# Two blocks with their layers written out, part of layer 2's modulation moved into layer 1, and the second block's first weights loaded inside the first block

## The reference

```
mod = silu(c) @ w_mod[l] + b_mod[l]          # 6 vectors of 1024: shifts, scales, gates
h = rms_norm(x) * (1 + sc_m) + sh_m
x = x + g_m * mixer(h)                       # projections w_in, three branches, w_out
u = rms_norm(x) * (1 + sc_f) + sh_f
x = x + g_f * (routed experts(u) + shared expert(u))   # 64 experts, top 8 of 4 groups
```

## Time and profile before

| | |
|---|---|
| median of the runs | 2278.68 us (2278.5 to 2287.8) |
| the profiled execution's own time | 2280.89 us |
| its span | 2279.2 us, 1.7 us less |
| PE busy | 2142.2 us (94%) |
| mean granted TensorE clock | 0.978 |
| DVE, ACT, POOL busy | 976.2, 512.4, 59.3 us |
| moved by DMA | 599.17 MB, mean 263 GB/s |

### The profile page before, as it was taken

One profiled execution on the slowest core, in us unless ns is written; L12 is line 12 of the kernel. 1 busy time (PEld: TensorE's weight loads), 2 busy tenths in 40 slices (PEclk: granted clock), 3 DMA queues, 4 the chain that ended last, 5 costly groups with the idle time before them and its releaser, 6 DMA issues. The chain is left out here.

```text
span 2279.2 us, 35703 instructions
## 1 busy us (share of the span) xinstructions
PE 2142.2 (94%) x13338; PEld 1243.4 (55%) x13405; DVE 976.2 (43%) x2063; ACT 512.4 (22%) x1080; POOL 59.3 (3%) x143
## 2 busy tenths in 40 slices
PE   4999998899999999979999988999999998799998
PEld 2844444556565655547454445565565654366475
DVE  2574323444444444337634144444444444152153
ACT  2133111122222222223232111222222222113122
POOL 1000002000000000000000030000000000110000
PEclk8999999999999999989999999999999999798999
DMA  8652734599999999876536427999999994731621
GB/s 290 207 208 91 295 111 166 213 380 380 388 370 387 379 383 379 323 281 194 194 109 250 178 119 282 382 374 387 377 383 380 382 384 186 244 97 39 221 67 55
DMA packets 165292, 599.17 MB, mean 263 GB/s; under 512 B 13052, under 2 KB 17760, under 8 KB 130656
## 3 DMA queue, kind: packets, MB, share of 16 engines
q1 hardware_dynamic: 163808, 595.10, 68.9%
q0 software_dynamic: 1408, 3.10, 0.6%
HBM read 597.11 MB, written 1.05 MB: 262 GB/s over the span
## 5 line engine op out<-in xcount | busy, mean ns | idle before, releaser
L1103 PE MATMUL banks<-weight_ring,h_t 128*64 128x256 f32 x4224 | 481.8, 381 | 3.3 <-DVE h_t L1836 3.3
L1103 PEld LDWEIGHTS banks<-weight_ring,h_t 128*64 128x64 f32 x4224 | 298.4, 137 | 173.9 <-issue 40.0
L769 PE MATMUL banks<-weight_ring,h_t 128*128 128x512 f32 x768 | 335.8, 593 | 5.3 <-DMA weight_ring<-in_w_in 3.2
L769 PEld LDWEIGHTS banks<-weight_ring,h_t 128*128 128x128 f32 x768 | 145.1, 190 | 188.1 <-issue 182.9
L1862 DVE SCALAR_TENSOR_TENSOR conv_t<-banks,slot_weight,xn 128x512 f32<-128x512 f32 x132 | 99.2, 751 | 293.6 <-ACT xn L1397 293.6
L1091 PEld LDWEIGHTS banks<-z,sp_ 128*128 128x128 bf16 x3168 | 180.5, 99 | 57.2 <-issue 49.2
L1091 PE MATMUL banks<-z,sp_ 128*128 128x128 bf16 x3168 | 202.7, 221 | 6.4 <-DVEq L1826 6.4
L1143 PE MATMUL banks<-xn,conv 128*128 128x512 bf16 x726 | 169.5, 382 | 9.2 <-DVE xn L1867 5.8
L1397 ACT ACTIVATE xn<-banks,slot_weight 128x512 bf16<-128x512 f32 x132 | 90.7, 687 | 342.8 <-PE banks L1130 342.8
L2103 PE MATMUL banks<-weight_ring,h_t 128*128 128x512 f32 (+2 forms) x384 | 136.7, 516 | 11.2 <-DMA weight_ring<-in_w_in 9.6
L1842 DVE TENSOR_TENSOR z<-banks,z 128x128 f32<-128x128 f32 x132 | 38.5, 292 | 229.8 <-ACT z L1382 229.8
(11 more groups left out here) (471 smaller groups left out, 2071.2 us busy)
## 6 DMA issues: line engine op xcount, KB each, us to landing
weight_ring<-in_w SPq DMA_DIRECT2D x264, 1024.0 KB, 10.5
weight_ring<-in_w_in SPq DMA_DIRECT2D x36, 2048.0 KB, 12.9
slots<-in_w SPq DMA_DIRECT2D x68, 1024.0 KB, 8.2
weight_ring<-in_w_mod SPq DMA_DIRECT2D x24, 2048.0 KB, 10.0
qk<-in_w SPq DMA_DIRECT2D x32, 1024.0 KB, 7.0
z<-in_w SPq DMA_DIRECT2D x32, 1024.0 KB, 11.5
weight_ring<-in_w_out SPq DMA_DIRECT2D x8, 2048.0 KB, 7.8
weight_ring<-in_w_in SPq DMA_DIRECT2D x10, 1024.0 KB, 7.8
```

Of the source, the lines that this page charges most:

```text
L769: mm = nc.tensor.matmul(bank[:, 0:cols], stationary[:, k, t * P:(t + 1) * P], w[:, k, 0:cols], start=(k == 0), stop=(k == KT - 1))
L1103: mm = nc.tensor.matmul(h_bank[g * SLOTS:(g + 1) * SLOTS, 0:FF], x_blk[:, j // 2, k, own], w13(j)[:, :, k, g * (FF // 2):(g + 1) * (FF // 2)],
```

## The change

1. All layer loops are written out (`for l in range(DEPTH)`), so that what a wait compares with is a constant. Bank and slot semaphores are shared by both blocks; the 16 increments at the second block's start are gone.
2. Lists are made per layer. `w_mod` chunks 0 to 3 of layer 2 (named 12 to 15) are loaded and used at the end of layer 1: part 12 ahead of `mT`, part 13 behind it, sum 12 and part 14 behind `wo`, sum 13 and part 15 behind the turn, sums 14 and 15 behind `rt`. DVE folds 12 and 13 behind `modulate(1)`, 14 and 15 in the middle of the routing. Layer 2 starts with `ug`.
3. The parameters are in three groups: `load_mod_params` (6 loads) behind `mod` 3, `load_conv_params` (4) behind `ua`, `load_other_params` (10) behind `kc`; layer 2's are issued in layer 1 behind the last `expert2` ahead of the experts' loop. The `vec` turn stands behind `ua`, DVE's `lam` lines behind the stick-breaking part, and the waits are split accordingly.
4. The second block's first four chunks (5 loads, since `n0` has two halves) are issued at the end of the first block's SP program, each when `h_done` says that the last experts have left its slot.
5. The shared expert's first product no longer waits for all four banks; the first layer's `block_count` has three register loads instead of five.

```diff
@@ bank_plan, lists
+MOD_NEXT = {"merged": [("part", 12)], "mT": [("part", 13)], "wo": [("sum", 12), ("part", 14)],
+            "turned": [("sum", 13), ("part", 15)], "rt": [("sum", 14), ("sum", 15)]}
+def chunks_1(layer):
+    first, following = layer == 0, layer + 1 < DEPTH
+    return (
+        mod_chunks(*range(MOD_FIRST if first else 0)) + [(n, (n, 1)) for n in ("ug", "ua", "qc", "kc")]
...
+        + branch_chunks(0) + branch_chunks(1) + mod_chunks(*((12, 13) if following else ()))
+        + [(("wo", h), ("wo", h, 1)) for h in range(2)] + mod_chunks(*((14, 15) if following else ())) + [("shared", None)]
+    )
@@ first_block, SP
-            with sp.Fori(0, DEPTH) as l:
+            for l in range(DEPTH):
                 one = ds(l, 1)
-                pairs_before = [sp.value_load(K.pairs_before[0:1, i, ds(l, 1)], ...
+                if l > 0:
+                    pairs_before = [sp.value_load(K.pairs_before[0:1, i, ds(l, 1)], ...
...
                     if name == ("mod", MOD_FIRST - 1):
-
-                        parameters(one)
+                        load_mod_params(one)
+                    if name == "ua" and l == 0:
+                        load_conv_params(one)
+                    if name == "kc" and l == 0:
+                        load_other_params(one)
...
                 expert2(l, 3, 3)
+                if l + 1 < DEPTH:
+
+                    sp.wait_ge(chosen_ready.sem, chosen_ready.at(l))
+                    sp.sem_inc(wait_carrier, 1)
+                    load_mod_params(ds(l + 1, 1))
+                    load_conv_params(ds(l + 1, 1))
+                    load_other_params(ds(l + 1, 1))
...
+            for s in range(RING):
+
+                sp.wait_ge(h_done, (pairs_before[0] + pairs_before[1]) * 2 + (s % 2 + RING - 1))
+                load_chunk_2(sp, A, K, 0, CHUNKS_2[s][0], s)
@@ first_block, PE
                 mod("start")
 
-                pe.wait_ge(params.sem, params.at(l, params.n))
-                bank = begin("vec", l)
...
                 norm_turn(0, l)
...
+                by_columns("ug")
+                by_columns("ua")
+
+                pe.wait_ge(conv_params.sem, conv_params.at(l, conv_params.n))
+                bank = begin("vec", l)
...
+                mod("merged")
                 pe.wait_ge(merged_ready.sem, merged_ready.at(l))
...
+                mod("mT")
                 pe.wait_ge(mt_ready.sem, mt_ready.at(l))
...
+                mod("wo")
                 norm_turn(1, l)
+                mod("turned")
                 pe.wait_ge(ht_ready[1].sem, ht_ready[1].at(l, 3))
+                pe.wait_ge(other_params.sem, other_params.at(l, other_params.n))
...
+                mod("rt")
@@ first_block, DVE
                 norm_x(0, l)
-                mod(range(MOD_FIRST))
-
-                dve.wait_ge(params.sem, params.at(l, params.n))
+                if l == 0:
+                    mod(range(MOD_FIRST))
+
+                dve.wait_ge(mod_params.sem, mod_params.at(l, mod_params.n))
                 mod_columns(0)
                 modulate(0, l)
...
                 modulate(1, l)
+                if l + 1 < DEPTH:
+                    mod((12, 13))
                 dve.wait_ge(score_ready.sem, score_ready.at(l))
...
+                if l + 1 < DEPTH:
+                    mod((14, 15))
                 v.tensor_tensor(g_score[:], top[:, :, :, 0], top[:, :, :, 1], ALU.add)
@@ second_block, SP
-            for b in range(BANKS):
-                sp.sem_inc(free[b].sem, 1)
-                sp.sem_inc(full[b].sem, full[b].credit)
             sp.sem_inc(vn_ready.sem, 1)
-            with sp.Fori(0, DEPTH) as l:
+            for l in range(DEPTH):
...
+                    if l > 0 or before is not None:
+                        load_chunk_2(sp, A, K, l, name, s)
```

More of the change, by code:

```diff
@@ L358, with mod_steps, mod_groups @@
-GROUPS_1 += ["-pad"] * (-len(GROUPS_1) % BANKS)
+MOD_NEXT = {"merged": [("part", 12)], "mT": [("part", 13)], "wo": [("sum", 12), ("part", 14)],
+            "turned": [("sum", 13), ("part", 15)], "rt": [("sum", 14), ("sum", 15)]}
+def mod_steps(place, layer):
+    if place == "start" and layer > 0:
+        return []
+    if place in MOD_NEXT:
+        return MOD_NEXT[place] if layer + 1 < DEPTH else []
+    return MOD_STEPS[place]
+def mod_groups(place, layer):
+    return [("mod_" + what, c) for what, c in mod_steps(place, layer)]
@@ L641, in _ @@
[L641 to L646 removed]
+                    load(lam4[:, i, :], A[name][one].to_broadcast([P, DA_HD]), other_params)
+                load(subln[:], A["subln_g"][one].to_broadcast([P, 2 * DA_HD]), other_params)
@@ L1454, in _ @@
             v.memset(more_below[:], 0.0)
-            with dve.Fori(0, DEPTH) as l:
+            for l in range(DEPTH):
                 one = ds(l, 1)
@@ L1908, in _ @@
                     dve.drain().then_inc(x_out.sem, 1)
+        return ([f.n for f in full], [f.n + 1 for f in free]), arrived
 HEADS_2 = MLA_H + MOBA_H
@@ L1990, in seg @@
             return nat[:, :, NAT[name]:NAT[name] + n]
-        B, full, free = bank_plan(GROUPS_2, K.psum, sem, "2")
-        filled = [Signal(sem(f"slot{s}_filled2")) for s in range(RING)]
+        B, _, _ = bank_plan(GROUPS_2, K.psum, (K.bank_full, K.bank_free), banks_before)
+        filled = [Signal(K.slot_filled[s], credit=slots_before[s]) for s in range(RING)]
         names = [c[0] for c in CHUNKS_2] + [("wo", 0), ("wo", 1)]
@@ L2065, in _ @@
         def _(pool):
-            with pool.Fori(0, DEPTH) as l:
+            for l in range(DEPTH):
                 pool.wait_ge(vn_ready.sem, vn_ready.at(l, 0))
@@ L2112, in turn @@
                 mm.then_inc(B[name].full, 1)
-            with pe.Fori(0, DEPTH) as l:
+            for l in range(DEPTH):
                 def natural(name):
@@ L2261, in pairs @@
                 return bank[:].rearrange("p (c n) -> p c n", c=2)
-            with act.Fori(0, DEPTH) as l:
+            for l in range(DEPTH):
                 for t in range(T):
@@ L2623, in build @@
         K.psum = [psum[:, b] for b in range(BANKS)]
-        first_block(nc, A, K)
-        second_block(nc, A, K, out)
+        K.bank_full, K.bank_free = ([ctx.enter_context(nc.semaphore(f"bank{b}_{what}")) for b in range(BANKS)]
+                                    for what in ("full", "free"))
+        K.slot_filled = [ctx.enter_context(nc.semaphore(f"slot{s}_filled")) for s in range(RING)]
+        banks_before, slots_before = first_block(nc, A, K)
+        second_block(nc, A, K, out, banks_before, slots_before)
 INPUTS = [
```

374 lines of the change are left out of this document (204 added, 170 removed).

## The result

| | before | changed |
|---|---|---|
| median of the runs | 2279.62 us (2278.5 to 2287.8, 4 runs) | 2240.81 us (2238.45 to 2242.32, 4 runs) |
| ratio, 95% interval | | 0.9829 (0.9808 to 0.985) |
| profiled execution, its span | 2280.89, 2279.2 us | 2242.32, 2240.6 us |
| mean granted clock | 0.978 | 0.985 |

The account below looks back on a forecast made before the run. PE bounds the experts, DMA close behind; the change targets three gaps where PE idles. Terms sum to -29.2 us, from 2280.9 to 2251.7; the median lies 2.2 lower, 2249.5, called 2250, range 2240 to 2265.

Parts of the forecast that it names:

- Start: Kernel's start to the first projection: earlier first load and fewer parameter loads to wait for, -9.3 us (ends -6.5 and -11).
- Layer 1's tail: End of layer 1 up to its experts: moved parts and sums mostly fill gaps, -2.2 us (ends -4 and +6).
- Layer 1 to 2: DVE's last addition in layer 1 to layer 2's first projection: PE starts at 993.3 instead of 1005.90, -12.6 us.
- End of layer 2: Last `pair_add` of layer 2: slower with the next chunks in flight, as at layer 1's end, +3.1 us.
- Second block: Step from first to second block: the chunk wait ends and the turn decides, PE starts at 1949.4, -7.8 us.
- The loops' ends in block 2: Second block: the one loop end left out there saves 0.4 us.
- the slower one: Rival, chance 0.04: in the experts' loop copies the jump back costs a fetch, some 29 turns give +41, 2291 us.
- The moved work: Rival, chance 0.12: moved work shows in layer 1's tail, which costs +8 instead of -2 us, giving 2260.
- the chunks do nothing: Rival, chance 0.03: at the second block early chunks are held until the block's end or stay behind `norm_g`, 2257 us.
- The late starts that go with a packet of code: Rival, chance 0.12: at both steps an engine's code is missing while the ring loads, 3.5 us each, 2257 us.

Follow-up runs that it names:

- n3: Changed kernel with all small parameter loads again in one stretch behind modulation group 3, waits for all ahead of the first projections: 2246.94 us.
- n5: Changed kernel with early chunks, early modulation and parameter split all undone, leaving written-out layers and four smaller parts: 2258.02 us, ratio 0.9887 to the kernel before.
- n2: Changed kernel with layer 2's modulation computed inside layer 2 again, none of it during layer 1: 2244.64 us.
- n1: Changed kernel with the second block's first four weight chunks loaded in the second block again: 2247.78 us.
- after_again: Changed kernel without any edit, profiled and timed again: 2240.61 us.
- d0: Kernel before with six clearings of a scratch tile added on DVE at the second block's start: 2282.28 us against 2285.32, ratio 0.9988.
- d2: Changed kernel with six clearings of a scratch tile added on DVE at the second block's start: 2243.61 us.
- b_again: Kernel before without any edit, profiled a second time: 2274.73 us, span 2273.1.
- n4: Changed kernel with two of the second block's chunks loaded early instead of four: 2238.1 us, timed again 2238.78.

## Why the prediction was right, and where its sum was off

- **Start, -9.3 forecast.** Measured -7.9 (A), and 40.0 to 43.5 us in the traces with the split, where about 40.6 was forecast. The chain behind the last fold is as worked out: DVE from 38.83, the projection at 42.08. What was mis-sized is DMA's part: the first chunk is issued 2.5 us earlier (3.88), not 1.6, but the last one is used only 1.9 earlier and its part took 3.06 us at a low clock, so the last fold ended 0.2 earlier, not 1.6. Then 1.6 us go back in stage B (n3), which the sum left out.
- **Layer 1's tail, -2.2 forecast.** From the last branch product to the first expert block it took 84.9 us before and 85.4 after: +0.5. Right were the router at the upper clock (3.79 us), the shared product of 13.9, the shorter register loads (the gap of 3.74 is 2.33) and the folds, 0.69 and 1.08 us with no block from POOL. Right was the DMA wait at `wo` too: the chunk landed 7.8 us after its issue, where 7.3 were taken, and `wo` came 2.4 us later behind the last branch product than before, where 1.8 were forecast. Up to the end of the shared product the tail is 0.5 us shorter, with 0.9 forecast; behind it, it is 1.0 longer, with 1.3 less forecast. Not foreseen was a new low stretch from 402 to 410 there, in which eight matmuls took 5.78 us; eight like them took 3.60 before.
- **Layer 1 to 2, -12.6 forecast.** From DVE's last addition to the projection 19.4 us became 6.6: -12.8. The size was right because the step was rebuilt from the work that stays. What pays for it was not told apart. With the layers only written out this step takes 13.9 us (n5), so that 5.5 of the 12.8 are the straight code's and 7.3 the modulation's move's. Over the whole stage E the straight code brings 8.6 and the move 5 to 6; the move gives 4.0 back in layer 1, which makes it worth 3.8 us in all (n2).
- **End of layer 2, +3.1 forecast.** In the first trace +4.4 (idle 4.04, then 5.30 us at a low clock), in the second +1.5, all of it low clock, with no more idle time than before. **This step failed**: the rows of before, one at each layer's end, were read as an effect of the loads in flight, and as a fixed price. At layer 1's end loads are in flight in all thirteen traces, and the idle time is between 2.17 and 3.58 us. What goes with the late starts is a late packet of code (last section), 0.5 to 1.9 us each time. The Trainium skill (Runtime: NRT & Kernel Launch, "Instruction fetch mechanics") says that a taken branch out of the current window forces a fetch; these packets agree with it, and with no fixed price.
- **Second block, -7.8 forecast.** From turn to product 13.2 us became 5.0, the whole step -8.5 and, taken back, +8.2 (n1 against after_again). d0 and d2 show what bound it before and what does now.
- **The loops' ends in block 2, -0.4 forecast. This term was mis-sized**, and the clock behind it was put at nothing: H fell by 11.7 us. 7.3 of it are the low stretch from 2074, in the execution that the forecast was made from and not in the next. 2.7 are the first product, 30.41 us before at a partly low clock, 27.73 after. 1.5 are the step between the block's two layers, where the loop turned: the turn comes 0.6 us and the product another 0.9 sooner, and the turn ran at a partly low clock in both traces of before. Against the second trace of before H fell by 4.4. The rows of this step, in b_again and in after_again (there the turn's first half):

```profile
2113.75 3.53 PE L2140 MATMUL banks<-ident,xn 128*128 128x128 f32 x16 [2.52 <-DVEq L2411]
```

```profile
2080.74 1.16 PE L2246 MATMUL banks<-ident,xn 128*128 128x128 f32 x8 [1.95 <-DVEq L2517]
```

The sum missed by 9.4 us (2251.7 against 2242.3). Its last term missed by 11.3; the rest, -28.8 in the sum, measured -26.9 (38.6 less H's 11.7). Part of that agreement is luck: the five terms themselves came to -24.3 (-7.9, +0.5, -12.8, +4.4, -8.5), and stage F's -3.3 belong to none of them. Luck too is the result's place in the range. The ends given for the single terms add up to -37.2 and -12.9, not to -41.8 and -16.3 (with the second block's low end, which is not given, at its -7.8), and the measured -38.6 lies outside of them. From the second trace of before (span 2273.1) the same sum gives 2243.9, and the changed kernel's two spans are 2240.6 and 2239.0.

Of the rivals, the slower one fell: stage D is 540.14 us against 539.88, so the expert loop's copies cost nothing. The moved work cost layer 1 4.0 us (n2), which other parts of the change nearly made good: the tail grew by 0.5 in all, where the rival had 8. That the chunks do nothing is refuted by n1. The late starts that go with a packet of code cost 1.7 to 1.9 us at layer 2's end in three of the ten traces of written-out kernels and 0.5 to 0.7 at layer 1's end in two, where that rival had 3.5 at each of two places.

## What to carry to other kernels

Rebuild a gap from the work that remains, and then ask separately what each part of a change would give alone: here a step came out right to 0.2 us, and over two fifths of its gain came from another edit than the move that was made for it. Writing the loops of two turns out, with the small changes that n5 keeps, was worth 27 us of 2285, more than the three moves that it made possible. In the traces 10 us of it lie at the places where the loops turned and 7 in one stretch of low clock that the kernel before does not always show. A stall that a single trace shows once is not a price: profile the same kernel twice before a term is built on it.

## What the runs showed of the hardware that was not expected

- **The clock granted to the same code differs between executions.** Of 29 executions of the kernel before that were timed beside the experiments, six had a mean clock of 0.979 or more and took 2275.65 to 2278.42 us; the other 23 had 0.972 to 0.976 and took 2282.63 to 2290.09. The low stretch in block 2 costs 7.3 us and is there in two of the three traces of this code (before and d0, not b_again). That it is what divides the two groups is not shown: the profiled execution of before, which has it, took 2280.89 us at 0.978 and lies between them, as do three of d0's ten runs.
- **The written-out kernels hardly show it.** The changed kernel's nine runs lie at 0.984 to 0.987, and none of the ten traces of written-out kernels has that stretch (n4 has 1.4 us at 2078). With the busy time of PE as weight, low clock cost 36.4 us in the trace of before, 28.8 in its second, 39.6 in d0, and 20.4 to 25.4 in the ten. PE's instructions ahead of the stretch are the same in all; what calls it up in the looped kernel stays open.
- **A product that starts before the clock is back up gives part of an earlier start back.** The 64 matmuls of block 2's first product took 27.73 us in the five traces in which the clock rose ahead of them and 29.39 to 30.47 in the other eight. n4's product began 5.8 us earlier than the changed kernel's (1924.50 against 1930.27) and took 2.2 longer.
- **A late start of `pair_add` goes with a late packet of code.** The traces record packets of the kind `instruction`. In the changed kernel's first trace one of 16 KB runs from 1906.30 to 1907.35, while `pair_add` stands idle until 1909.14. The DMA view from 1906.2 to 1907.4 (queue, kind: packets, MB, share):

```profile
q8 instruction: 1, 0.02, 5.5%
```

Thirteen traces have 26 last `pair_add`s of a layer. In the eight with more than 2.18 us of idle time a 16 KB packet of this queue ended 1.6 to 1.8 us ahead of the start; in the other 18 none ended between 0.8 and 2.5 us ahead. So the wait is most likely one for code. Why the packet comes late in one execution and not in the next is open: the eight all had loads in flight, at 382 to 392 GB/s, but so had 13 of the other 18.
